# Mixture-of-experts stage of a two-block network: next group's rows transposed one group earlier, scatter behind the weight strips, two copies of the transposed picks

## The reference, cut to what matters

```python
def hier_moe(h, w_rg, b_rg, w_re, b_re, w_gate, w_up, w_down):
    g_logits = (xf @ w_rg + b_rg)            # 4 groups, top 1
    ...
    top_v, top_i = lax.top_k(e_in_group, 2)  # 2 of the 8 experts of that group
    ...
    for e in range(32):
        hid = jax.nn.silu(xf @ w_gate[e]) * (xf @ w_up[e])   # 1024 -> 128
        y = y + combine[:, e:e + 1] * (hid @ w_down[e])      # 128 -> 1024
```

## Time and profile before

| | us |
|---|---|
| median of 3 runs | 968.56 |
| lowest, highest | 968.02, 970.27 |
| the profiled execution, its own time | 966.54 |
| its span, first to last instruction | 964.7 |
| TensorE busy | 802.8 (83%) |
| VectorE busy | 244.1 (25%) |
| ScalarE busy | 163.3 (17%) |
| mean granted TensorE clock | 0.936 |

### The profile page before, as it was taken

How to read it: one execution, slowest core, us unless ns; L and a number is a source line. 1 busy time by engine, 2 the same in 40 slices (tenths; PEclk the granted TensorE clock), 3 DMA queues, 4 the chain that set the end, 5 groups by cost and what they waited for, 6 DMA issues and landing times.

```text
span 964.7 us, 20303 instructions
## 1 busy us (share of the span) xinstructions
PE 802.8 (83%) x9043; PEld 548.2 (57%) x9043; DVE 244.1 (25%) x637; ACT 163.3 (17%) x345; POOL 64.1 (7%) x71
## 2 busy tenths in 40 slices
PE   7999999999899889999998877767566675665765
PEld 4565688874665544446756665546346464553543
DVE  2142921231522221433535221201102020110201
ACT  2112222320411122204724010001000010000100
POOL 8000300000000030160000000000000000000000
PEclk9999999999999999999999998888889797879877
DMA  9986533066699999442636999999999999999995
GB/s 259 373 300 213 200 117 145 1 271 252 251 402 416 411 398 366 185 174 88 238 135 251 423 425 427 426 430 428 427 431 427 430 427 427 431 427 431 427 429 246
DMA packets 55118, 312.64 MB, mean 324 GB/s; under 512 B 4744, under 2 KB 5984, under 8 KB 42784
## 3 DMA queue, kind: packets, MB, share of 16 engines
q1 hardware_dynamic: 50688, 301.86, 77.9%
q0 software_dynamic: 2912, 6.96, 2.1%
q10 hardware_dynamic: 1472, 3.15, 0.8%
HBM read 307.76 MB, written 4.19 MB: 323 GB/s over the span
## 4 chain that ended last, share of the span: by engine, by line
PE 56%; DMA 37%; DVE 3%; issue 2%; ACT 1%; SPq 0%; DVEq 0%; ACTq 0%
PE ps L1598 53%; DMA ring<-in_w_up 19%; DMA ring<-in_w_down 10%; DMA ring<-in_w_gate 7%; DMA ring<-in_w_in 1%; PE ps L1624 1%; PE ps L1773 1%; PE ps L1908 0%; PE ps L2007 0%; PE ps L1655 0%; PE ps L1735 0%; ACT arena L859 0%; DVE xx L1078 0%; PE ps L1813 0%; DVE arena L1330 0%
## 5 line engine op out<-in xcount | busy, mean ns | idle before, releaser
L1598 PE MATMUL ps<-ring,arena 128*32 128x128 f32 (+3 forms) x5824 | 283.1, 338 | 138.1 <-DMA ring<-in_w_up 46.5
L1598 PEld LDWEIGHTS ps<-ring,arena 128*32 128x32 f32 (+1 forms) x5824 | 196.9, 124 | 220.5 <-issue 82.2
L1598 PE MATMUL ps<-ring,xx 128*128 128x512 f32 (+2 forms) x384 | 157.8, 568 | 0.0
L1598 PE MATMUL ps<-arena 32*128 32x256 f32 (+11 forms) x1360 | 127.8, 368 | 4.9 <-ACT arena L859 1.2
L1598 PEld LDWEIGHTS ps<-ring,xx 128*128 128x128 f32 x384 | 72.6, 192 | 76.0 <-issue 72.3
L1598 PEld LDWEIGHTS ps<-arena 32*128 32x128 f32 (+4 forms) x1360 | 80.3, 167 | 35.8 <-issue 28.4
L849 ACT ACTIVATE arena<-ps 128x128 f32<-128x128 f32 x40 | 11.1, 277 | 456.4 <-PE ps L1598 456.4
L1294 DVE TENSOR_TENSOR arena<-arena,ps 128x128 f32<-128x128 f32 x40 | 11.5, 288 | 296.0 <-ACT arena L849 296.0
L1598 PE MATMUL ps<-xx,ring 128*128 128x256 f32 x288 | 64.9, 382 | 0.0
L1598 PEld LDWEIGHTS ps<-xx,ring 128*128 128x128 f32 x288 | 53.8, 190 | 7.9 <-issue 0.7
L1598 PE MATMUL ps<-ring,xs 128*128 128x512 f32 x96 | 42.0, 594 | 1.0 <-DMA ring<-in_w_in 1.0
(11 more groups left out here) (289 smaller groups left out, 558.6 us busy)
## 6 DMA issues: line engine op xcount, KB each, us to landing
ring<-in_w_up SPq DMA_DIRECT2D x37, 2048.0 KB, 25.3
ring<-in_w_down SPq DMA_DIRECT2D x37, 2048.0 KB, 24.0
ring<-in_w_gate SPq DMA_DIRECT2D x36, 2048.0 KB, 23.7
ring<-in_w_in SPq DMA_DIRECT2D x15, 2048.0 KB, 20.3
ring<-in_w_out SPq DMA_DIRECT2D x4, 2048.0 KB, 8.2
arena<-in_w_gate SPq DMA_DIRECT2D x3, 2048.0 KB, 12.1
arena<-in_w_up SPq DMA_DIRECT2D x3, 2048.0 KB, 16.6
arena<-in_w_down SPq DMA_DIRECT2D x3, 2048.0 KB, 11.2
```

The lines of the kernel that those rows point to most:

```text
L1598: ins = pe.matmul(dst, w, x, start=start, stop=stop, skip_group_check=True)
```

## The change

TensorE prepares group n + 1 (its rows, or its gather) inside group n, behind the hidden transpose and ahead of the down matmuls. The transposes of the picks and the first half of the scatter move behind the up strips, the second half behind the prepared rows. `pick_T` has two copies, so ScalarE's copy no longer waits for the scatter (`s_grp` is gone), and comes ahead of the copy of the hidden tile. VectorE's `gathered` for the next group stands behind the token cast. Group 7 prepares a group 8 too, whose rows nobody reads. The loop of TensorE waits at its end for `s_xg`. The diff, cut to its core:

```diff
-        pick_T = kb(10, T)
+        pick_T = [kb(10, T), kb(16, T)]
...
-                def group(n):
+                def group(n, half):
                     n1 = act.snap(n + 1)
                     gate(n1, 0)
+                    act.wait_ge(s_ptp[0], n1)
+                    act.activation(pick_T[half], bank(5, T), ACT.Copy).then_inc(s_pkT[0], 1)
                     act.wait_ge(s_ht[0], n1)
                     act.activation(hid[:, 0, :], bank(4, P), ACT.Copy).then_inc(s_hid[0], 1)
-                    act.wait_ge(s_ptp[0], n1)
-                    act.wait_ge(s_grp[0], n1)
-                    act.activation(pick_T, bank(5, T), ACT.Copy).then_inc(s_pkT[0], 1)
                     act.wait_ge(s_y[0], n1)
...
                 def group(n, r, c_next, half):
-                    gathered(n)
                     dve.wait_ge(s_posm[0], dve.snap(r + 1))
                     dve.wait_ge(s_pw, dve.snap(n + 1))
-                    pick_slots(0, dve.snap(c_next + EG), half)
+                    dve.wait_ge(s_xg[0], dve.snap(n * 2 + 2))
+                    pick_slots(0, c_next + EG if isinstance(c_next, int) else dve.snap(c_next + EG), half)
                     hidden(dve.snap(n + 1), 0)
                     dve.tensor_copy(token[:, half:half + 1], bank(7, 1, T)).then_inc(s_tok, 1)
+                    gathered(dve.snap(n + 1))
                     dve.wait_ge(s_ptp[0], dve.snap(n + 1))
...
+                def prepare(n, half, q):
                     if isinstance(n, int) and n < 2:
                         gather(n)
                     else:
-                        gathered_rows(parity, n // 2 if isinstance(n, int) else q)
-                    pe.wait_ge(s_pw, n1)
-                    pe.wait_ge(s_ysb_d[0], n1)
-                    pe.wait_ge(s_rounds, 1)
-                    for tt in range(TT):
-                        ins = pe.transpose(bank(5, P, tt * P), pick_w[:, tt, :], ident)
-                    ins.then_inc(s_ptp[0], 1)
-                    if not fresh:
-
-                        scatter(n1, pieces=(0, 1))
+                        gathered_rows(half, q)
+
+                def group(n, c, q, half, nth=0):
...
+                    if fresh:
+                        picks_transposed()
                     pe.wait_ge(s_xg[0], val(n * 2 + 2))
-                    pe.wait_ge(s_ysb_a[0], n1)
                     for i in range(2):
...
                     if not fresh:
-                        scatter(n1, pieces=(2,))
+                        picks_transposed()
+                        scatter(n1, 1 - half, pieces=(0, 1))
+                    pe.wait_ge(s_ysb_a[0], n1)
                     pe.wait_ge(s_h[0], n1)
                     pe.transpose(bank(4, P), hid_tm[:, 0], ident).then_inc(s_ht[0], 1)
+                    pe.wait_ge(s_tok, n1)
+                    prepare(val(n + 1), 1 - half, (n + 1) // 2 if isinstance(n, int) else pe.snap(q + half))
                     if not fresh:
-                        scatter(n1, pieces=(3,)).then_inc(s_grp[0], 1)
+                        scatter(n1, 1 - half, pieces=(2, 3))
                     arrived(c[2], q, nth)
...
                 if b == 0:
+                    gather(0)
                     group(0, FIRST1[0:3], 0, 0)
...
+                            pe.wait_ge(s_xg[0], pe.snap(r * (2 * NGRP) + g * 4 + 6))
```

More of the change, by code:

```diff
@@ L359, in program @@
         s_ysb_d = [sem(f"moe_down_out_by_dve{b}") for b in (0, 1)]
-        s_grp = [sem("moe_group_scattered0")]
         s_pkT_d = sem("moe2_picks_T_by_dve")
@@ L876, in moe @@
                             for half in range(2):
-                                group(act.snap(r * NGRP + g * 2 + half))
+                                group(act.snap(r * NGRP + g * 2 + half), half)
                         else:
@@ L1298, in gathered @@
                     for half in range(2):
-                        dve.wait_ge(s_xgp[b], dve.snap(n * 2 + (half + 1)))
+                        dve.wait_ge(s_xgp[b], n * 2 + half + 1 if isinstance(n, int) else dve.snap(n * 2 + (half + 1)))
                         gains = gcol[:, row + 4 * half:row + 4 * half + 4].unsqueeze(2).broadcast_to([P, 4, P])
@@ L1339, in group2 @@
                         dve.tensor_copy(y_exp[:, j % 2], bank(4 + j % 2, T)).then_inc(s_ysb_d[1], 1)
+                if b == 0:
+                    gathered(0)
                 with dve.Fori(0, rounds) as r:
@@ L1872, in moe, with scatter @@
                 pe.reg_mov(done, 0)
-                def scatter(n1, last=False, pieces=range(4)):
+                def scatter(n1, par, last=False, pieces=range(4)):
                     pe.wait_ge(s_ysb_a[0], n1)
@@ L1880, in scatter @@
                         tt, half = i // 2, i % 2
-                        ins = mm(bank(i), pick_T[:, tt * P:(tt + 1) * P], y_sb[:, half * 512:half * 512 + 512],
+                        ins = mm(bank(i), pick_T[par][:, tt * P:(tt + 1) * P], y_sb[:, half * 512:half * 512 + 512],
                                  False, False)
@@ L1942, in group, with picks_transposed @@
                     else:
-                        gathered_rows(parity, n // 2 if isinstance(n, int) else q)
-                    pe.wait_ge(s_pw, n1)
-                    pe.wait_ge(s_ysb_d[0], n1)
-                    pe.wait_ge(s_rounds, 1)
-                    for tt in range(TT):
-                        ins = pe.transpose(bank(5, P, tt * P), pick_w[:, tt, :], ident)
-                    ins.then_inc(s_ptp[0], 1)
-                    if not fresh:
-                        scatter(n1, pieces=(0, 1))
+                        gathered_rows(half, q)
+                def group(n, c, q, half, nth=0):
+                    n1 = val(n + 1)
+                    fresh = isinstance(n, int) and n == 0
+                    def picks_transposed():
+                        pe.wait_ge(s_pw, n1)
+                        pe.wait_ge(s_ysb_d[0], n1)
+                        pe.wait_ge(s_rounds, 1)
+                        for tt in range(TT):
+                            ins = pe.transpose(bank(5, P, tt * P), pick_w[:, tt, :], ident)
+                        ins.then_inc(s_ptp[0], 1)
+                    if fresh:
+                        picks_transposed()
                     pe.wait_ge(s_xg[0], val(n * 2 + 2))
-                    pe.wait_ge(s_ysb_a[0], n1)
                     for i in range(2):
@@ L1958, in group @@
                         if i == 1:
-                            slot_tokens(n, parity)
+                            slot_tokens(n, half)
                         ins = strips(6 + i, lambda k, j: xg[:, k, j * SLOTS:(j + 1) * SLOTS],
@@ L1975, in group @@
                     w = slot3(c[2], EG, D)
-                    for half in range(2):
+                    for part in range(2):
                         for j in range(EG):
-                            ins = mm(bank(4 + half)[32 * j:32 * j + 32], hid[:, 0, 32 * j:32 * j + 32],
-                                     w[:, j, half * 512:half * 512 + 512], True, True)
+                            ins = mm(bank(4 + part)[32 * j:32 * j + 32], hid[:, 0, 32 * j:32 * j + 32],
+                                     w[:, j, part * 512:part * 512 + 512], True, True)
                     ins.then_inc(s_y[0], 1)
@@ L2036, in moe @@
                         group(n, AHEAD1[n], 0, n % 2, n // 4)
+                    pe.wait_ge(s_xg[0], 2 * 6 + 2)
                 else:
@@ L2055, in moe @@
                 if b == 0:
-                    scatter(pe.snap(pe.snap(done) * NGRP + 1), last=True)
+                    scatter(pe.snap(pe.snap(done) * NGRP + 1), 1, last=True)
                 else:
```

## The result

| | before | after |
|---|---|---|
| median of 20 runs, us | 968.35 | 971.39 |
| lowest, highest | 963.68, 970.27 | 966.94, 974.12 |
| profiled execution, its own time | 966.54 | 969.03 |
| its span | 964.7 | 967.2 |
| mean granted clock | 0.936 | 0.927 |

The ratio is 1.0031, with a 95% interval from 1.002 to 1.0041: the change makes the kernel slower by 3 us (1.9 to 4.0).

What follows compares the result with a forecast made beforehand. The weight stream was taken to bound the first mixture's end. Group 7's down starts at 353.0 + 1.1 (clock) = 354.1 against 353.04, so 968.56 + 1.0 gives 969.6 us; range 966.7 to 971.7.

Steps and rivals of the forecast that it cites:

- the likeliest case: Longer end of group 7, with a fall of the clock: 969.6 us, own range 968.0 to 971.2; 62 in 100.
- the first case: The same forecast of a longer end of group 7: 969.6 us, 62 in 100.
- the fourth: Clock stays low over most of the 7.5 us behind group 7's up chunk, costing 3.2 us: 971.7; 15 in 100.
- What bounds the stage: End of first mixture: the weight stream sets the last landings; earlier-released chunks only wait longer in line.
- Waits removed on TensorE: Groups 0 to 7: about 5.3 us of idle removed, less 0.93 for group 8's rows; 4.4 us if TensorE were the bound.
- The stream: Hole near 268 closes, later landings come 0.85 us earlier; no new hole at group 3's down chunk.
- The end of group 7: 7.5 us of work behind the up chunk, against 5.1 before; down starts at 353.0, so removed waits are given back.
- I take the middle, 345.5: Group 7's up chunk lands between 345.05 (earlier stream) and 345.9 (pushed back by group 6's row fetch).
- The clock: TensorE waits 3 to 4.5 us for group 7's up chunk; the clock's fall costs 0 to 1.6 us.
- I take 1.1: Cost in us taken for the clock's fall at group 7's up chunk, out of 0 to 1.6.
- The step on the skill's rule: By the rule, the clock's fall in group 7 is certain and costs the full 1.6 us: 354.6 instead of 354.1.
- Rows ready in time: GpSimd's row fetch lands within at most 10.5 us, rows due 11.2 plus 2.1 us behind the same point; no cost.

Runs made afterwards that it cites:

- e4: The kernel before plus only the two copies of the transposed picks, copied by ScalarE ahead of the hidden tile; 1.0006 of the kernel before.
- e3: The changed kernel with each group's rows transposed at its own start as before, and no group 8; 1.0040 of the kernel before.
- e6: The changed kernel without the two row fetches of groups 6 and 7 for a second round (256-byte transfers instead); 1.0019 of the kernel before.
- e7: The kernel before without the two row fetches that only a second round would read; 0.9997 of the kernel before.
- e1: The changed kernel with three extra useless matmuls in groups 6 and 7 ahead of the wait for the up chunk; 1.0013 of the kernel before.
- e2: The changed kernel with picks' transposes and two scatter pieces moved between gate strips and the wait for the up chunk; 1.0015 of the kernel before.
- e5: The changed kernel with picks' transposes and three scatter pieces moved ahead of the wait for the up chunk; 1.0007 of the kernel before.
- e8: The changed kernel with three scatter pieces moved ahead of the up chunk's wait and no row fetches for a second round; 0.9986 of the kernel before.
- e10: The changed kernel with all four scatter pieces ahead of the up chunk's wait and no second-round row fetches; 966.59 us, 0.9981 of the kernel before.
- e9: The changed kernel without the eight transposes for a group 8, whose rows only a second round would read; 1.0028 of the kernel before.

## Why the prediction was right

The forecast of 969.6 us was for a loss of 1.0; measured is a loss of 3.0, inside the range but near its upper end of 971.7. The mechanism of the likeliest case came, with two of its terms too small. Three things limit what the hit says:

- The time, 971.39, lies above that case's own range (968.0 to 971.2), and the prediction had given a loss over 0.2% only 22 in 100. By size the result lies between the first case and the fourth ("slower"), nearer to the fourth.
- The 971.2 doesn't come out of the prediction's terms. A late up chunk at 345.9, 7.5 us and a full fall of 1.6 make 355.0, or 970.5; the other 0.7 us has no term.
- The count of the profiled executions, 3.96 us, would have put the kernel at 972.5, outside the range. That the medians fell inside is in part luck.

The steps, one by one:

- *What bounds the stage: right.* On the count the up chunk was issued 6.3 us earlier and landed 1.2 us later; e4 took 0.62 us out of each group and gained nothing.
- *Waits removed on TensorE: right.* No wait for a copy is left in groups 1 to 7.
- *The stream: the hole right, its effect on the last landing not shown.* The hole near 268 closed, none opened at group 3's down chunk (issued at 268.94, 15.8 on the count; the windows there show 373 to 422 GB/s), and over the 14 us from the count of 6 the stream moves 377 GB/s against 355, 0.3 MB or 0.75 us more. Group 7's down chunk landed 0.7 us earlier, 0.85 forecast. But the match may be luck: e3 and e4 issue group 3's up chunk as the kernel before does (11.7 on the count, 11.8 before, 10.4 after), and their down chunks land at 97.4 and 98.3. Without the last fetches the two orders differ by only 0.2 us (e6, e7). What else moves this landing is open.
- *The end of group 7: right in kind, and close in length.* 7.5 us were forecast from the landing at the higher clock, 7.1 measured in e1. But the up chunk landed at 92.5 on the count. The step "I take the middle, 345.5" stood for 90.9. It let the fetch take back half of the 0.85 us of the earlier stream. Measured, the fetch costs the up chunk 1.8 us in the new order (e6) against 0.5 us in the old (e7), and without the fetches the up chunk lands at 90.6 and 90.8, so the earlier stream hardly shows in it. Mis-sized by 1.6 us.
- *The clock: right in kind, too small in size.* "I take 1.1" was bounded by one strip pass, 1.6 us. The fall lasted from ahead of the landing to about 351, over strips, picks and a part of the scatter, and cost 2.7 us. Mis-sized by 1.6 us. The price of the fourth case, 3.2 us for two such passes, was nearer.
- The three differences, +1.6, +1.6 and -0.4, and 0.1 us from the landing to the first token matmul make up 102.4 against the forecast of 99.5 on the count (354.1 - 254.61).
- *The step on the skill's rule: misread.* The Trainium skill, "TensorE: Matmul & The Clock Gate", section "HAM oscillation — how this bites in real kernels", tells of bursts of matmuls shorter than the DMA wait behind them, each next one at the lower clock. The prediction took it to make the fall certain here. But ahead of the wait of 3.85 us TensorE had worked for 14.0 us (327.88 to 341.86), and longer still ahead of that of 2.53 us, so the rule's condition wasn't met, and the clock fell all the same. The length of the wait alone doesn't decide it: behind 2.53 us the clock fell, behind 2.37 us in e2 it did not, behind 2.20 us in e6 it did.
- *Rows ready in time: right.* No wait for a fetch appears.

## What to carry to other kernels

Where a stage ends with a stream of weights, list what has to run behind the landing of each of the last chunks; work that doesn't need the chunk belongs ahead of its wait, even if an order that puts it behind has no wait in the middle of the stage. A wait taken out of the engine that runs ahead of its data comes back in front of the last chunk, in one piece, and a wait in one piece can cost the clock as well. Here waits of 0.6 us spread over the groups left the clock up, and one wait of 3.85 us ahead of the last work cost 2.7 us more (e1 against the changed kernel). Where such a fall comes earlier and a wait for data as long as its cost still follows, as in group 6, it costs nothing.

## What the runs showed of the hardware

- Matmuls without use, 3.0 us of them in place of group 7's wait for its up chunk, made the kernel's stage 2.0 us shorter, although they ended 1.2 us too late (e1).
- A row fetch of half a megabyte, 1.3 us at 413 GB/s, delays the landing of group 7's up chunk by 0.5 us (before against e7), 1.3 us (e5 against e8) or 1.8 us (after against e6). The down chunk lands 1.8 us later with the fetches (after) or 2.3 us (before).
- In some profiled executions the clock falls behind the waits of 0.85 and 1.87 us at the start of block 2 and in others not, though the code from there on is the same. The first product takes 1.63 us (before, after, e1, e4, e6, e7, e8, e10) or 2.07 to 2.20 (e2, e3, e5, e9), and from it to the router's first product 148.1 to 148.3 us pass in place of 146.9. With one execution of each kernel it isn't shown whether the kernel or chance decides. From the first product to the end of the span are 601.3 to 603.3 us over all of them. Together with 4.8 us of spread in the start of the stage this is the size of the effects studied, so single profiles had to be compared by stage.
